# Index keys and key latents turned inside the second index query block, last fill units staged over early scores, low parts of the weights subtracted in quarters

## The chip, the cores and the metric
The kernel runs on one core of a Trainium2 chip. The metric is the device time of one execution in microseconds (us), the median of several runs. TensorE is called PE here, VectorE DVE, ScalarE ACT, GpSimd POOL and the queue of SyncE SP. PSUM (`ps`) is used as 8 banks of 128 x 512 float32.

## The reference
One decoder layer over 1024 tokens of width 1024: an attention branch and a state space branch side by side, merged, then an MLP. What matters here is the attention branch:

```
proj = h @ w_in          # q, kv_lat, q_idx, k_idx, w_idx, z, xbc, dt, g_att, g_ssd
c_kv  = rms_norm(kv_lat); k_idx = rms_norm(k_idx)
# per block of 128 queries:
score[t, s] = sum_h w_idx[t, h] * relu(q_idx[t, h] . k_idx[s])     # 8 heads of 64, causal
keep the 256 keys with the highest score of each query
softmax attention over the kept latents, k = c_kv W_uk, v = c_kv W_uv
```

The first two blocks of 128 queries see at most 256 keys and need no selection.

## The kernel before
Every large product is made of three matmuls in fp32r, hi x hi, hi x lo and lo x hi, where hi is a float32 rounded to fp32r and lo is what is left of it. So each weight block of 1024 x 256 is loaded by SP into `raw[s]` (two buffers, s = n % 2), POOL copies it to `w_hi[s]` (L576) and subtracts to get `w_lo[s]` (L578), and PE waits for both in `w_wait` (L642, semaphore `w_split`). PE gives the buffer back with `w_used`; SP loads the next block into `raw[s]` once `w_split` has counted the block before (L378). There are 90 such splits.

A feature-major block (`fm_block`, L648) runs over k = 0 to 7 with twelve 128x512 matmuls each into four banks. In order of PE's program, from 100 us on:
- the latents and the small columns by token (`kv_token`, `tm_token`), which DVE scales into `ckv_tm` and `kidx_tm`;
- two blocks of index queries, `fm_block(2, 0)` and `fm_block(3, 1)` (L729 to L731). ACT copies each head to `q_idx` (L1244) and DVE subtracts the low part into the other half of the partitions (L1690), in the order heads 0 to 3, keys, heads 4 to 7;
- 8 transposes of `kidx_tm` into banks 0 and 1 (L735), after the second block. ACT makes `k_idx` hi (L1241), DVE lo (L1685);
- four sixteenths of the first q block (`first_q_part`, L738) in banks 0 to 3, then the logits of the index (L756 to L770): ten groups of 8 heads in banks 4 to 7, each followed by another sixteenth. ACT takes the relu (L1252) into four `relu_buf` slots, DVE multiplies by the head's weight and adds up in `score` (L1703, L1705);
- 16 transposes of `ckv_tm` into banks 4 to 7 (L775), after the last relu; ACT makes `ckv_hi` (L1256), DVE `ckv_lo` (L1711) in front of its top-k; PE runs two more sixteenths and waits for them before the next block (L789);
- 15 more blocks for q, k, v, gates, B and C and half of the state space gate. ACT evacuates each two banks as a unit u into `spill[u % 4]` and stores it (`unit`, L1258). The last four, units 40 to 43, go to `last_spill`, which lies over the scores of blocks 4 to 7, so ACT waits with them until top-k has ended (L1297, released at L1802).

Meanwhile DVE runs top-k (L1755 to L1765): three pairs of query blocks, 32 rounds of max and match_replace each. Then attention starts on PE (L873 to L883): scores of head 0 for block t into `ps`, DVE adds the mask (L1781, into `prob`, whose first two buffers lie at 8 and 12 KB of the scores' place), ACT takes the exponential (L1310), PE transposes (L865) into `probT`, and so on. Between the first four positions stand the matmuls of the cumulated decay (L878, L879), whose results DVE takes at L1809, behind a wait for the last units' stores (L1807).

Later, at the end of the state space branch, DVE scales eight sums of squares (L1919), ACT takes the root (L1503), DVE scales `zy` (L1925) and PE turns it (`y_turn`, L889) amid the first output block, for which DVE also makes `a_lo` (L1852).

Of the kernel before, what the change touches and what calls it, by code (L numbers as in the profile page):

```python
# [60 lines left out]
def hybrid_block(nc, x, c, ada_w, ada_b, norm_g, w_in, kv_norm_g, kidx_norm_g, w_uk, w_uv, conv_w, conv_b,  # L61
# [51 lines left out]
    NC = DFF // WC  # L113
    N_ALL = N_MLP + 2 * NC

# [69 lines left out]
    last_spill = [place(f"last_spill{i}", [P, SEQ], F32, R1 + (16 + 4 * i) * K) for i in range(4)]  # L185
# [67 lines left out]
    with ctx:  # L253
# [103 lines left out]
        FREE_BLOCKS = TOPK // P  # L357
# [15 lines left out]
        def _(sp):  # L373
            def load(n, src, dst=None, turn=None, per=0):
                s = n % 2
                if n >= 2 or turn is not None:

                    sp.wait_ge(w_split[s], n // 2 + (0 if turn is None else turn * (per // 2)))  # L378
                dst = raw[s][:, :].rearrange(W3, c=WC) if dst is None else dst
                sp.dma_start(dst, src).then_inc(raw_in[s], 16)  # L380
# [162 lines left out]
        def _(pool):  # L543
# [94 lines left out]
        def _(pe):  # L638
# [3 lines left out]
            def w_wait(n, extra=0):  # L642
                pe.wait_ge(w_split[n % 2], n // 2 + 1 + extra)
# [108 lines left out]
            pe.wait_ge(qi_split, 5)  # L752
            w_wait(4)
            for part in range(4):
                first_q_part(part)
            part = 4  # L756
            pe.wait_ge(qi_split, 9)
            i = 0
            for b in range(FREE_BLOCKS, NT):
                for k0, n in logit_chunks(b):  # L760
                    for h in range(HI):
                        if i >= 4:
                            pe.wait_ge(relu_done, i - 3)
                        o = ps[:, 4 + i % 4, 0:n]
                        q_h = q_idx[:, h, b * P:(b + 1) * P]
                        mm(o, q_h, k_idx[0][:, k0:k0 + n], start=True)
                        mm(o, q_h, k_idx[1][:, k0:k0 + n], stop=True).then_inc(logit_done, 1)
                        i += 1
                    first_q_part(part)
                    part += 1  # L770

            pe.wait_ge(relu_done, LOGITS)
            for r in range(2):
                for t in range(NT):
                    last = nc.tensor.transpose(ps[:, 4 + 2 * r + t // 4, (t % 4) * P:(t % 4 + 1) * P],  # L775
                                               ckv_tm[:, t, r * P:(r + 1) * P], ident[:, :])
            last.then_inc(kv_turned, 1)
# [11 lines left out]
            pe.wait_ge(kv_out_split, 2)  # L789
# [84 lines left out]
            attend(0, range(2), 0)  # L874
# [5 lines left out]
            attend(0, range(2, 4), 0)  # L880
# [292 lines left out]
        def _(act):  # L1173
# [63 lines left out]
            for b in range(2):  # L1237
                act.wait_ge(w_used[b], 2)
                if b:
                    act.wait_ge(kv_turned, 1)  # L1240
                    nc.scalar.copy(k_idx[0][:, :].rearrange("p (a b) -> p a b", a=2), ps[:, 0:2, :]).then_inc(qi_out, 1)  # L1241
                for h in range(4 * b, 4 * b + 4):
                    half, src = q_source(h)
                    nc.scalar.copy(q_idx[half, h, FREE_BLOCKS * P:SEQ], src).then_inc(qi_out, 1)  # L1244
# [9 lines left out]
            act.wait_ge(kv_turned, 2)  # L1254
            for r in range(2):
                nc.scalar.copy(ckv_hi[:, r, :].rearrange("p (a b) -> p a b", a=2), ps[:, 4 + 2 * r:6 + 2 * r, :]).then_inc(kv_out, 1)  # L1256

            def unit(u, func, dst, turn=None, per=0):  # L1258
# [3 lines left out]
                if 4 <= u < 40 or turn is not None:  # L1262

                    act.wait_ge(spilled[b], 16 * (u // 4) + (0 if turn is None else turn * (4 * per)))
# [3 lines left out]
                act.dma_start(dst, stage[:, :]).then_inc(spilled[b] if u < 40 else last_spilled, 16)  # L1268
# [28 lines left out]
            act.wait_ge(topk_step, (NT // 2 - 1) * (2 + 4 * TOPK // 8) + 1)  # L1297
# [322 lines left out]
        def _(dve):  # L1620
# [60 lines left out]

            for n, h in enumerate((0, 1, 2, 3, None, 4, 5, 6, 7)):
# [4 lines left out]
                else:  # L1687
                    half, src = q_source(h)
                    other = slice(DI - half.start, 2 * DI - half.start)
                    ve.tensor_tensor(q_idx[other, h, FREE_BLOCKS * P:SEQ], src,  # L1690
                                     q_idx[half, h, FREE_BLOCKS * P:SEQ].bitcast(F32), ALU.subtract).then_inc(qi_split, 1)
# [17 lines left out]
            for r in range(2):  # L1709
                dve.wait_ge(kv_out, 2)  # L1710
                ve.tensor_tensor(ckv_lo[:, r, :].rearrange("p (a b) -> p a b", a=2), ps[:, 4 + 2 * r:6 + 2 * r, :],  # L1711
                                 ckv_hi[:, r, :].bitcast(F32).rearrange("p (a b) -> p a b", a=2), ALU.subtract).then_inc(kv_out_split, 1)

# [3 lines left out]

            rows8 = [P, NT, NS]

            def every_chunk(row):  # L1720
                return row[:, :].rearrange("p (o h) -> p o h", o=1).broadcast_to(rows8)

            V.link(ve.tensor_tensor(dt[:, :, :], dt[:, :, :], every_chunk(dtb_row), ALU.add))
# [78 lines left out]
            dve.sem_inc(topk_step, 1)  # L1802
# [3 lines left out]
            attend(0, range(2, 4), 0)  # L1806
            dve.wait_ge(last_spilled, 16 * 4)  # L1807
# [271 lines left out]
```

## Time and profile before

| what | value |
|---|---|
| median of 3 runs | 2447.12 us (2447.07 to 2447.74) |
| the profiled execution | 2445.2 us |
| its span, first to last instruction | 2443.5 us |
| PE busy | 2335.8 us (96%) |
| DVE busy | 1383.2 us (57%) |
| ACT busy | 721.9 us (30%) |
| POOL busy | 870.2 us (36%) |
| granted TensorE clock, mean | 0.991 of 2.4 GHz |

Times in rows are us from the span's start. Busy time counts instructions in work; a matmul's end is modelled, so two that follow closely overlap. "Idle before" is how long the engine stood before an instruction, and behind the arrow is what ended it.

### The profile page before, as it was taken

Reading aid. Unit: us, or ns where it says so; the run is one execution under the profiler, and the core shown is the slowest. Engines: PE = TensorE matmul, PEld = TensorE weight load, DVE = VectorE, ACT = ScalarE, POOL = GpSimd, SP = SyncE. Lnnn points to the kernel's source line nnn. Section 1 sums busy time; section 2 is a strip of 40 time slices with the busy share of each in tenths; the row PEclk is TensorE's granted clock in tenths of the full one; section 3 lists DMA queues with packets and bytes.
Section 4 is the critical chain, followed back from the end, with each engine's and each line's share of the span. In section 5 each row is a group of like instructions: output and inputs, shape, how many; then the busy total and the mean of one; then the engine's idle time right before and its main releaser. Section 6 shows DMA issues by size and latency. Waiting matters only on the chain.

```text
span 2443.5 us, 31678 instructions
## 1 busy us (share of the span) xinstructions
PE 2335.8 (96%) x12022; PEld 1927.4 (79%) x12022; DVE 1383.2 (57%) x1956; ACT 721.9 (30%) x1360; POOL 870.2 (36%) x360
## 2 busy tenths in 40 slices
PE   3999999998999999999999999999999999999997
PEld 2977878884557988888877788899888888888886
DVE  4249999995657267685867565544632231322315
ACT  5144121105652234434365111034511211212112
POOL 1221233226671352634445233235323322333232
PEclk9999999999999999999999999999999999999999
DMA  7111452215652113141223443334211111111103
GB/s 270 36 35 39 151 181 90 99 61 177 206 165 72 40 61 125 50 141 40 85 102 125 148 145 133 120 104 138 87 52 52 46 40 51 51 51 34 51 34 78
DMA packets 144729, 230.25 MB, mean 94 GB/s; under 512 B 7956, under 2 KB 111732, under 8 KB 143604
## 3 DMA queue, kind: packets, MB, share of 16 engines
q1 hardware_dynamic: 119936, 166.11, 20.7%
q10 hardware_dynamic: 23684, 59.06, 6.3%
q0 software_dynamic: 1008, 3.67, 0.8%
q8 instruction: 71, 1.16, 0.2%
q14 instruction: 30, 0.25, 0.0%
HBM read 176.39 MB, written 52.43 MB: 94 GB/s over the span
## 4 chain that ended last, share of the span: by engine, by line
PE 71%; issue 12%; DVE 11%; ACT 3%; DVEq 1%; DMA 1%; ACTq 0%
PE ps L646 69%; DVE score L1703 2%; DVE score L1765 1%; DVE top L1761 1%; DVE c_out L1873 1%; DVE probT L1798 1%; DVE mod_sum L1641 1%; DVE x_tm L1980 1%; PE ps L865 1%; DVEq L1755 1%; PE ps L964 0%; PE ps L897 0%; DVE a_lo L1631 0%; ACT decay L1490 0%; DVEq L1763 0%
## 5 line engine op out<-in xcount | busy, mean ns | idle before, releaser
L646 PE MATMUL ps<-a_hi,w_hi 128*128 128x512 f32 x1728 | 679.0, 393 | 6.7 <-DVE k_idx_lo L1685 2.4
L646 PE MATMUL ps<-a_lo,w_hi 128*128 128x512 f32 x1728 | 674.8, 391 | 0.0
L576 POOL CAST w_hi<-raw 128x2048 fp32r<-128x2048 f32 x90 | 176.7, 1964 | 1276.2 <-PE ps L646 1045.0
L646 PE MATMUL ps<-a_hi,w_lo 128*128 128x512 f32 x1728 | 544.6, 391 | 0.0
L578 POOL TENSOR_TENSOR w_lo<-raw,w_hi 128x2048 fp32r<-128x2048 f32 x90 | 431.8, 4798 | 7.2
L2009 DVE TENSOR_TENSOR x_tm<-x_tm,ps 128x1024 f32<-128x1024 f32 x120 | 146.6, 1221 | 453.7 <-PE ps L646 453.1
L646 PEld LDWEIGHTS ps<-a_hi,w_hi 128*128 128x128 f32 x1728 | 325.4, 188 | 76.4 <-issue 3.0
L646 PEld LDWEIGHTS ps<-a_hi,w_lo 128*128 128x128 f32 x1728 | 325.4, 188 | 68.1
L646 PEld LDWEIGHTS ps<-a_lo,w_hi 128*128 128x128 f32 x1728 | 325.6, 188 | 65.8
L646 PE MATMUL ps<-w_hi,a_hi 128*128 128x256 f32 (+1 forms) x896 | 260.8, 291 | 8.5 <-ACTq L1547 4.8
L646 PE MATMUL ps<-w_lo,a_hi 128*128 128x256 f32 (+1 forms) x896 | 255.2, 285 | 0.0
L646 PE MATMUL ps<-w_hi,a_lo 128*128 128x256 f32 (+1 forms) x896 | 255.0, 285 | 0.0
L646 PE MATMUL ps<-w_lo,u_hi 128*128 128x512 f32 x512 | 204.5, 399 | 0.0
L646 PE MATMUL ps<-w_hi,u_hi 128*128 128x512 f32 x512 | 202.0, 394 | 0.0
L646 PE MATMUL ps<-w_hi,u_lo 128*128 128x512 f32 x512 | 200.8, 392 | 0.0
L1596 ACT ACTIVATE u_tmp<-ps 128x512 f32<-128x512 f32 x64 | 37.9, 593 | 522.9 <-PE ps L646 522.9
L646 PEld LDWEIGHTS ps<-w_hi,a_hi 128*128 128x128 f32 x896 | 173.9, 194 | 10.7 <-ACTq L1547 5.0
L646 PEld LDWEIGHTS ps<-w_lo,a_hi 128*128 128x128 f32 x896 | 174.0, 194 | 1.4 <-issue 1.4
L646 PEld LDWEIGHTS ps<-w_hi,a_lo 128*128 128x128 f32 x896 | 174.0, 194 | 0.0
L1765 DVE MATCH_REPLACE8 score<-top,score 128x384 f32<-128x384 f32 (+2 forms) x192 | 166.5, 874 | 0.0
L1761 DVE MAX8 top<-score 128x8 f32<-128x384 f32 (+2 forms) x192 | 160.9, 878 | 0.0
L646 PEld LDWEIGHTS ps<-w_hi,u_hi 128*128 128x128 f32 x512 | 96.2, 188 | 24.9
(255 smaller groups left out, 3094.6 us busy)
## 6 DMA issues: line engine op xcount, KB each, us to landing
raw<-in_w_in_dram SPq DMA_DIRECT2D x35, 1024.0 KB, 5.3
ada_raw<-in_ada_w_dram SPq DMA_DIRECT2D x16, 1024.0 KB, 8.7
raw<-in_w_up_dram SPq DMA_DIRECT2D x16, 1024.0 KB, 5.7
raw<-in_w_down_dram SPq DMA_DIRECT2D x16, 1024.0 KB, 4.8
gates<-gate_d SPq DMA_DIRECT2D x12, 1024.0 KB, 4.9
act_raw<-acts_d ACTq DMA_DIRECT2D x20, 512.0 KB, 5.1
ada<-in_ada_w_dram SPq DMA_DIRECT2D x8, 1024.0 KB, 21.3
acts_d<-decay ACTq DMA_DIRECT2D x16, 512.0 KB, 3.9
```

The source lines that it names most:

```text
L576: nc.gpsimd.tensor_copy(hi, src).then_inc(hi_made, 1)
L578: nc.gpsimd.tensor_tensor(lo, src, hi.bitcast(F32), ALU.subtract).then_inc(w_split[s], 1)
L646: return nc.tensor.matmul(o, a, b, start=start, stop=stop)
L865: ins = nc.tensor.transpose(ps[:, 4 + turns % 2, (k % 4) * P:(k % 4 + 1) * P], prob[(t - 3) % 4][:, k * P:(k + 1) * P], ident[:, :])
L1596: nc.scalar.activation(u_tmp[j][:, :], ps[:, banks[j], :], ACT.Relu).then_inc(up_out, 1)
L1641: V.link(ve.scalar_tensor_tensor(mod_sum[:, :], ada0[:, k, :], c_act[:, k:k + 1], mod_sum[:, :], ALU.mult, ALU.add))
L1703: ins = ve.scalar_tensor_tensor(s, r, w, s, ALU.mult, ALU.add)
L1755: with dve.Fori(0, ROUNDS) as i:
L1761: ve.max(top8[j][:, :], pair[j]).then_inc(topk_step, 1)
L1765: ve.match_replace(pair[j], top8[j][:, :], pair[j], TAKEN).then_inc(topk_step, 1)
L1798: ve.tensor_copy(probT[g % 2][:, k0:k0 + m, q0:q0 + P], ps[:, 4 + turns % 2, 0:m * P].rearrange("p (k q) -> p k q", k=m)).then_inc(pt_out, 1)
L2009: ins = ve.tensor_copy(o, part) if first else ve.tensor_tensor(o, o, part, ALU.add)
```

## The change
Four things are changed.
- PE turns the keys and the first half of the latents at k = 3 of the second index query block, and the second half at k = 5, into banks 0 to 3, which the first block has left. ACT and DVE make their high and low parts before heads 4 to 7. The 16 transposes, copies and subtractions behind the logits are gone. `q_idx` keeps only the queries from 256 on, `ckv_hi` moves and `ckv_lo` lies in the first 8 KB of the scores' place, which the scores of blocks 0 and 1 would take and nobody uses.
- Two sixteenths of the first q block stand ahead of the logits instead of four, and PE waits for the banks of heads 4, 5 and 6, 7 apart.
- Units 40 and 41 are staged over the scores of blocks 2 and 3, units 42 and 43 over `ckv_lo`'s place; ACT waits only until top-k's first pair of blocks is through. DVE waits for the stores of 40 and 41 in front of attention, and for those of 42 and 43 in front of its fourth position; PE runs three positions ahead of the decay matmuls instead of two.
- POOL subtracts `w_lo` in four instructions of a quarter each, and all counts of `w_split` are times four. The sum of dt and its bias moves to a place before the index heads.

```diff
+    LO_PARTS = 4
-    q_idx = place("q_idx", [P, HI, SEQ], F32R, R2)
-    ckv_hi = place("ckv_hi", [P, 2, SEQ], F32R, R2 + 16 * K)
-    ckv_lo = place("ckv_lo", [P, 2, SEQ], F32R, R2 + 24 * K)
+    FREE_BLOCKS = TOPK // P
+    q_idx = place("q_idx", [P, HI, SEQ - TOPK], F32R, R2)
+    ckv_hi = place("ckv_hi", [P, 2, SEQ], F32R, R2 + 24 * K)
+    ckv_lo = place("ckv_lo", [P, 2, SEQ], F32R, R1)
-    last_spill = [place(f"last_spill{i}", [P, SEQ], F32, R1 + (16 + 4 * i) * K) for i in range(4)]
+    last_spill = [place(f"last_spill{i}", [P, SEQ], F32, R1 + (8, 12, 0, 4)[i] * K) for i in range(4)]
...
-                nc.gpsimd.tensor_tensor(lo, src, hi.bitcast(F32), ALU.subtract).then_inc(w_split[s], 1)
+                for j in range(LO_PARTS):
+                    c = slice(j * width // LO_PARTS, (j + 1) * width // LO_PARTS)
+                    nc.gpsimd.tensor_tensor(lo[:, c], src[:, c], hi[:, c].bitcast(F32), ALU.subtract).then_inc(w_split[s], 1)
...
-            for b in range(2):
-                pe.wait_ge(kv_read, b + 1)
-                fm_block(2 + b, b).then_inc(w_used[b], 1)
-            pe.wait_ge(qi_split, 4)
-            for t in range(NT):
-                last = nc.tensor.transpose(ps[:, t // 4, (t % 4) * P:(t % 4 + 1) * P], kidx_tm[:, t, :], ident[:, :])
-            last.then_inc(kv_turned, 1)
+            def kv_turns(k):
+                if k == 3:
+                    pe.wait_ge(qi_split, 4)
+                    for t in range(NT):
+                        nc.tensor.transpose(ps[:, t // 4, (t % 4) * P:(t % 4 + 1) * P], kidx_tm[:, t, :], ident[:, :])
+                if k == 5:
+                    pe.wait_ge(qi_split, 5)
+                if k in (3, 5):
+                    r = (k - 3) // 2
+                    for t in range(NT):
+                        last = nc.tensor.transpose(ps[:, 2 - 2 * r + t // 4, (t % 4) * P:(t % 4 + 1) * P],
+                                                   ckv_tm[:, t, r * P:(r + 1) * P], ident[:, :])
+                    last.then_inc(kv_turned, 1)
+            pe.wait_ge(kv_read, 1)
+            fm_block(2, 0).then_inc(w_used[0], 1)
+            pe.wait_ge(kv_read, 2)
+            fm_block(3, 1, act_ready=kv_turns).then_inc(w_used[1], 1)
...
-            pe.wait_ge(qi_split, 5)
+            pe.wait_ge(kv_out_split, 2)
             w_wait(4)
-            for part in range(4):
+            for part in range(2):
                 first_q_part(part)
-            part = 4
-            pe.wait_ge(qi_split, 9)
+            part = 2
...
+                        elif i % 2 == 0:
+                            pe.wait_ge(qi_split, 7 + i)
...
-            pe.wait_ge(relu_done, LOGITS)
-            for r in range(2):
-                for t in range(NT):
-                    last = nc.tensor.transpose(...)
-            last.then_inc(kv_turned, 1)
...
-            pe.wait_ge(kv_out_split, 2)
+            pe.wait_ge(relu_done, LOGITS)
             fm_block(5, 1).then_inc(w_used[1], 1)
...
-            attend(0, range(2), 0)
+            attend(0, range(3), 0)
...
-            attend(0, range(2, 4), 0)
+            attend(0, range(3, 4), 0)
...
-            act.wait_ge(topk_step, (NT // 2 - 1) * (2 + 4 * TOPK // 8) + 1)
+            act.wait_ge(topk_step, 2 + 4 * TOPK // 8 + 1)
...
-            dve.sem_inc(topk_step, 1)
+            for b in range(2):
+                dve.wait_ge(spilled[b], 16 * 11)
             attend(0, range(2), 0)
             for b in range(2, 4):
                 dve.wait_ge(spilled[b], 16 * 10)
-            attend(0, range(2, 4), 0)
-            dve.wait_ge(last_spilled, 16 * 4)
+            attend(0, range(2, 3), 0)
+            dve.wait_ge(last_spilled, 16 * 2)
+            attend(0, range(3, 4), 0)
```

## Rows read from the trace of the kernel before

**Rows 1.** Busy table by stretch: length, engines' busy us (instructions), PE clock, DMA share, GB/s
```profile
core 0: us, PE busy (x) PEld busy (x) DVE busy (x) ACT busy (x) POOL busy (x), PEclk, DMA share, GB/s
127.00:149.00 22.00, 22.00 (x100) 18.17 (x99) 3.82 (x4) 3.19 (x4) 6.50 (x2) 1.00 0.15 48
...
227.00:549.00 322.00, 321.25 (x1410) 264.21 (x1408) 321.48 (x589) 45.25 (x44) 91.29 (x28) 1.00 0.32 117
549.00:559.00 10.00, 1.70 (x5) 0.93 (x4) 5.49 (x13) 4.09 (x4) 4.45 (x2) 0.76 0.92 322
```
**Rows 2.** Waits of PE: who waited for whom, us in total, times, longest
```profile
PE ps L646 <- ACT last_spill L1265: 8.3, 2, 7.1
```
**Rows 3.** Chain that ended last, around 149 us: start, us, what
```profile
149.01 0.89 PE ps L735 x8
```
**Rows 4.** Timeline of PE: start, us, engine, line, operation, out<-in, idle before
```profile
152.29 0.50 PE L646 MATMUL ps<-a_hi,w_hi 128*128 128x512 f32 x1 [2.42 <-DVE k_idx_lo L1685]
...
157.88 0.34 PE L646 MATMUL ps<-k_idx_hi,q_idx 128*128 128x384 f32 x1
...
213.24 1.97 PE L775 MATMUL ps<-ident,ckv_tm 128*128 128x128 f32 x16 [0.84 <-ACT relu_buf L1252]
...
219.68 0.50 PE L646 MATMUL ps<-a_hi,w_hi 128*128 128x512 f32 x1 [1.71 <-DVE ckv_lo L1711]
...
548.66 0.39 PE L646 MATMUL ps<-a_hi,w_lo 128*128 128x512 f32 x1
...
556.14 0.58 PE L646 MATMUL ps<-hk,hq 128*128 128x128 f32 x1 [7.09 <-ACT last_spill L1265]
...
569.42 0.70 PE L646 MATMUL ps<-hk,hq 128*128 128x512 f32 x1 [2.08 <-DVE att_stat L1784]
```
**Rows 5.** Timeline of ACT (first row) and DVE, 150 to 226 us
```profile
150.88 3.25 ACT L1244 CAST q_idx<-ps 64x768 fp32r<-64x768 f32 x4
...
152.27 3.91 DVE L1690 TENSOR_TENSOR q_idx<-ps,q_idx 64x768 fp32r<-64x768 f32 x4
158.96 0.42 DVE L1705 TENSOR_SCALAR score<-relu_buf,w_idx 128x384 f32<-128x384 f32 x1 [2.77 <-ACT relu_buf L1252]
159.48 4.95 DVE L1703 SCALAR_TENSOR_TENSOR score<-relu_buf,w_idx,score 128x384 f32<-128x384 f32 x7
...
210.03 5.88 DVE L1703 SCALAR_TENSOR_TENSOR score<-relu_buf,w_idx,score 128x512 f32<-128x512 f32 x7
...
220.33 4.72 DVE L1724 SCALAR_TENSOR_TENSOR acum<-dt 128x256 f32<-128x256 f32 x1
...
225.68 0.49 DVE L1753 TENSOR_TENSOR score<-score,future 128x128 f32<-128x128 f32 x2
```
**Rows 6.** Timeline of POOL, then its group of 128x512 additions (xcount, busy us, mean ns)
```profile
151.14 4.60 POOL L578 TENSOR_TENSOR w_lo<-raw,w_hi 128x2048 fp32r<-128x2048 f32 x1
...
220.10 4.68 POOL L578 TENSOR_TENSOR w_lo<-raw,w_hi 128x2048 fp32r<-128x2048 f32 x1
...
L597 POOL TENSOR_TENSOR ada_raw<-ada_raw 128x512 f32<-128x512 f32 x16 | 20.4, 1272 | 1.3
```
**Rows 7.** Timelines of DVE, ACT, DVE from 552 us; landing of last_spill's stores
```profile
552.16 1.36 DVE L1770 TENSOR_SCALAR bias_bf<-score 128x896 bf16<-128x896 f32 x2
...
557.95 1.02 ACT L1265 ACTIVATE last_spill<-ps 128x1024 f32<-128x1024 f32 x1 [0.42 <-ACT last_spill L1265]
...
564.28 0.69 DVE L1781 CUSTOM_DVE_ANT_0 prob<-ps,bias_bf 128x512 f32<-128x512 f32 x1 [0.79 <-PE ps L646]
...
DMA to landing us min/median/max: 3.3/3.6/3.9
```
**Rows 8.** Timelines of DVE, POOL and PE, 1333 to 1350 us
```profile
1337.25 4.57 DVE L1919 TENSOR_SCALAR stat<-stat 128x8 f32<-128x8 f32 x1
1344.37 1.23 DVE L1852 TENSOR_TENSOR a_lo<-act_raw,a_hi 128x1024 fp32r<-128x1024 f32 x1 [2.55 <-ACT a_hi L1383]
...
1336.33 5.47 POOL L578 TENSOR_TENSOR w_lo<-raw,w_hi 128x2048 fp32r<-128x2048 f32 x1
...
1349.11 1.30 PE L897 MATMUL ps<-ident,zy 128*128 128x128 f32 x5 [7.00 <-issue]
```

More of the change, by code:

```diff
@@ L355, in logit_chunks @@
             return [(i * n // parts, n // parts) for i in range(parts)]
-        FREE_BLOCKS = TOPK // P
         LOGITS = HI * sum(len(logit_chunks(b)) for b in range(FREE_BLOCKS, NT))
@@ L376, in load @@
                 if n >= 2 or turn is not None:
-                    sp.wait_ge(w_split[s], n // 2 + (0 if turn is None else turn * (per // 2)))
+                    sp.wait_ge(w_split[s], (n // 2 + (0 if turn is None else turn * (per // 2))) * LO_PARTS)
                 dst = raw[s][:, :].rearrange(W3, c=WC) if dst is None else dst
@@ L642, in w_wait @@
             def w_wait(n, extra=0):
-                pe.wait_ge(w_split[n % 2], n // 2 + 1 + extra)
+                pe.wait_ge(w_split[n % 2], (n // 2 + 1 + extra) * LO_PARTS)
             def mm(o, a, b, start=False, stop=False):
@@ L1238, in _ @@
                 act.wait_ge(w_used[b], 2)
-                if b:
+                for h in range(4 * b, 4 * b + 4):
+                    half, src = q_source(h)
+                    nc.scalar.copy(q_idx[half, h, :], src).then_inc(qi_out, 1)
+                if b == 0:
                     act.wait_ge(kv_turned, 1)
                     nc.scalar.copy(k_idx[0][:, :].rearrange("p (a b) -> p a b", a=2), ps[:, 0:2, :]).then_inc(qi_out, 1)
-                for h in range(4 * b, 4 * b + 4):
-                    half, src = q_source(h)
-                    nc.scalar.copy(q_idx[half, h, FREE_BLOCKS * P:SEQ], src).then_inc(qi_out, 1)
+                    for r in range(2):
+                        act.wait_ge(kv_turned, r + 1)
+                        nc.scalar.copy(ckv_hi[:, r, :].rearrange("p (a b) -> p a b", a=2), ps[:, 2 - 2 * r:4 - 2 * r, :]).then_inc(kv_out, 1)
             i = 0
@@ L1253, in _ @@
                         i += 1
-            act.wait_ge(kv_turned, 2)
-            for r in range(2):
-                nc.scalar.copy(ckv_hi[:, r, :].rearrange("p (a b) -> p a b", a=2), ps[:, 4 + 2 * r:6 + 2 * r, :]).then_inc(kv_out, 1)
             def unit(u, func, dst, turn=None, per=0):
@@ L1261, in unit @@
                 stage = spill[b] if u < 40 else last_spill[b]
-                if 4 <= u < 40 or turn is not None:
+                if 4 <= u < 42 or turn is not None:
                     act.wait_ge(spilled[b], 16 * (u // 4) + (0 if turn is None else turn * (4 * per)))
@@ L1267, in unit @@
                 act.wait_ge(unit_out, u + 1 + (0 if turn is None else turn * per))
-                act.dma_start(dst, stage[:, :]).then_inc(spilled[b] if u < 40 else last_spilled, 16)
+                act.dma_start(dst, stage[:, :]).then_inc(spilled[b] if u < 42 else last_spilled, 16)
             def fm_units(n, u, func, dst, turns):
@@ L1680, in _, with every_chunk @@
             ins.then_inc(kv_read, 1)
+            rows8 = [P, NT, NS]
+            def every_chunk(row):
+                return row[:, :].rearrange("p (o h) -> p o h", o=1).broadcast_to(rows8)
+            dve.wait_ge(kv_read, 2)
+            V.link(ve.tensor_tensor(dt[:, :, :], dt[:, :, :], every_chunk(dtb_row), ALU.add))
             for n, h in enumerate((0, 1, 2, 3, None, 4, 5, 6, 7)):
@@ L1689, in _ @@
                     other = slice(DI - half.start, 2 * DI - half.start)
-                    ve.tensor_tensor(q_idx[other, h, FREE_BLOCKS * P:SEQ], src,
-                                     q_idx[half, h, FREE_BLOCKS * P:SEQ].bitcast(F32), ALU.subtract).then_inc(qi_split, 1)
+                    ve.tensor_tensor(q_idx[other, h, :], src, q_idx[half, h, :].bitcast(F32), ALU.subtract).then_inc(qi_split, 1)
+                if h is None:
+                    for r in range(2):
+                        dve.wait_ge(kv_out, r + 1)
+                        ve.tensor_tensor(ckv_lo[:, r, :].rearrange("p (a b) -> p a b", a=2), ps[:, 2 - 2 * r:4 - 2 * r, :],
+                                         ckv_hi[:, r, :].bitcast(F32).rearrange("p (a b) -> p a b", a=2), ALU.subtract).then_inc(kv_out_split, 1)
             i = 0
@@ L1708, in _ @@
             dve.wait_ge(relu_used, LOGITS)
[L1709 to L1712, printed above, removed]
             ROUNDS = TOPK // 8
[L1718 to L1723, printed above, removed]
             ve.scalar_tensor_tensor(acum[:, :, :], dt[:, :, :], -1.0, dt[:, :, :], ALU.mult, ALU.max).then_inc(dt_abs, 1)
```

4 lines of the change are left out of this document (1 added, 3 removed).

## The prediction
> **What bounds the kernel now.** I read the table of busy time by stretch first, then the waits of TensorE (PE), then the chain and the engines' rows around each wait. PE works 321.25 of the 322 us from 227 to 549, so a change pays only where it stands still, and it stands for most of 549 to 559 [rows 1]. The waits name the causes [rows 2, 4]: 8.3 us for the last staged fill units, 2.4 for the low part of the index keys, 1.7 for that of the key latents. The longest single one comes at the end of the block: PE runs its last matmul until 549.05 and starts attention at 556.14, 7.09 us later [rows 4]. The cause is two steps back. DVE's top-k ends at 552.16 + 1.36 = 553.52; ScalarE (ACT) may copy the last four units only then, since they are staged where the scores lie, and takes them at 1.45 us each until 558.97; attention's fourth score block is masked at 564.28 and PE has a steady feed from 569.42 [rows 4, 7]. Two chains end here close together: DVE's (logits, top-k) at 553.5 and PE's (projections) at 549.05. The change shortens both, and the later one decides.
>
> **Index block.** The 8 key transposes (0.89 us) and 16 latent transposes (1.97) [rows 3, 4] move into the block that runs from 127.3 to 149.0. They stay PE work, so the block ends at 149.01 + 0.89 + 1.97 = 151.87. ACT's and DVE's copies of what they turn fall into this block, of whose 22 us they work 3.2 and 3.8 [rows 1]. The wait at k = 3 (about 135.4) needs q heads 0 to 3, whose low parts are done 4.8 us into the block, by 132.1. That at k = 5 (about 142.7) needs the keys' low part, which comes the 2.4 us of today's wait behind the turns, by 140. Both cost nothing; without that cover k = 5 would cost up to those 2.4 us. Nothing else is queued behind them on PE but the block itself. The waits of 2.42, 0.84 and 1.71 on PE disappear.
> After 151.87 ACT copies heads 4 to 7 (0.81 each) and DVE subtracts (0.98 each) [rows 5], one copy behind: heads 4, 5 are ready at 154.7, all at 156.65. PE meanwhile does two q parts; four of them ran from 152.29 until the first logit at 157.88, so 1.40 each [rows 4]. So it starts logits 0 and 1 at 154.7 and waits some 1.3 us for the rest. DVE could then start its scores at 156.7 instead of 158.96, 2.26 us sooner.
>
> It will hardly do so. GpSimd (POOL) splits the next weights as soon as this block ends; its low part ran from 151.14 for 4.60 us, 2.1 us behind the block's end [rows 6], and moves to 154.0. Such an instruction holds off DVE: the 128x256 scalar_tensor_tensor that began at 220.33, inside POOL's 220.10 + 4.68, took 4.72 us, and 8 elements at 1337.25 took 4.57, until POOL was done [rows 5, 6, 8]. In quarters of 1.27 [rows 6] (about 1.2 from start to start) the third runs until 157.65, so the first score is done at 158.0; the fourth then goes first, until 159.2; the second score ends at 159.85, against 160.1 before. Gain of DVE's stream: 0.25 us, between 0 (all four quarters ahead) and 2.26 (no collision); I take 0.25, since the rows show the collision. The Trainium skill, SBUF — State Buffer, section "Who interferes with whom", says that a VectorE instruction with two SBUF inputs, or in a 2-port mode, and a GpSimd one lock each other out for the whole instruction, whichever came first. By that rule, which the 4.72 us bears out, the start at 156.7 is lost; without it the whole forecast would be 1.8 us lower.
>
> From here DVE sets the pace (scores back to back until 210.03 + 5.88 = 215.91 [rows 5]), so the whole phase moves by 0.25. Then PE's path: its last logit ended at 213.24 - 0.84 - 1.40 = 211.0, now 210.75. Five q parts are left instead of three (two first instead of four), 7.0 us, so the next block starts at 217.8 against 219.68 [rows 4]: 1.9 gained. The work up to 549.05 has no slack [rows 1], so PE's projections end at **547.15**.
> DVE's path: from the last score at 215.91 to the first top-k row at 225.68 it spends 9.77 us [rows 5], of which the latents, the dt sum (now earlier, in an idle stretch) and the 4.72 go. Left are acum, by estimate 0.45 (384 elements take 0.62 of such an instruction, the first seven scores 4.95 between them), since POOL's split starts only with the next block, and the bias writes with 225.68 - 225.05 = 0.63: 1.1. So 8.65 + 0.25 sooner, and top-k ends at **544.6**. PE's chain is the later by 2.5 us.
>
> **Last units.** Units 40 and 41 are now staged over scores that the first top-k pair has finished, 42 and 43 over the dead latents; ACT no longer waits for top-k's end. 40 and 41 go out during the last block; their added wait is for stores of a block before. 42 and 43 follow at 547.2 and 548.65, the store of 43 is issued at 549.7 and lands 3.3 to 3.9 us later [rows 7], at 553.35. New behind that: DVE waits for units 42 and 43 ahead of the fourth mask, with ACT's fourth exponential, the decay sums and the masks 5 and on queued behind it. PE can compute its scores from 547.2; the fourth, after the two sums, is there by 552 at the full clock, so the landing is last. Mask 4 starts at 553.35 against 564.28 [rows 7]: **10.9 us gained**. From there to the steady feed it is the same 5.14 us (569.42 - 564.28), ACT, DVE and PE in turn. Bounds: 9.3 if ACT's shift alone carried through (unit 43 from 557.95 to 548.65), 12.8 if the score stream got its 2.26. SP's ada loads start with the block's end, 1.9 us sooner, and attention 10.9 sooner, so POOL's ada sums lose 9 us of their lead; no wait for them stands in today's list on PE, and I take the lead to be long enough.
>
> **Quarters.** Per split, 4 x 1.27 - 4.6 = about 0.4 us more on POOL, some 90 times, beside PE blocks of 149.0 - 127.3 = 21.7 us (half, 11 us, in the output projection, whose blocks have half the columns) of which cast and low part take 2.1 + 4.6 [rows 6]: hidden; it would cost PE only past some 4 us a split. Where DVE has four or more blocked instructions in a row (conv, x1), POOL takes every other turn and the stall is the same in sum: 0. One border gains. At 1337.25 DVE stands 4.57 us behind the low part that really began at 1337.2 (the 5.47 from 1336.33 include the wait for DVE) [rows 8]; with quarters it stands 1.3, 3.3 less. The next subtraction, which ran from 1344.37 to 1345.6, would come at 1341.1 [rows 8], meets the last quarter there, waits until 1342.2 and ends at 1343.5. So PE's wait, 7.00 us until 1349.11, ends 2.1 sooner; bounds 0 (alternation eats it) and 3.3. I take **2.1**.
>
> **Sum.** 10.9 + 2.1 = 13.0. The profiled execution took 2445.2 us (span 2443.5), 1.9 under the median of 2447.1; against it the changed one would be 2432.2, and the median **2434.1**.
>
> **Rivals.**
> - **A slow clock at the new seam.** The granted clock averages 0.76 in 549 to 559 after PE's idle 7 us [rows 1], so part of it is at 1.2 instead of 2.4 GHz. Now PE has small pieces and waits of 1 to 2 us from 547 to 558.5; if the clock falls late in this stretch, the dense work behind it runs at half speed. For: in the rows PE starts dense work only at 569.42 - 10.9. Against: its idle is in pieces. Price 2 to 5 us: 2437.5. 18%. The Trainium skill, TensorE: Matmul & The Clock Gate, part 1, calls the lower clock the default, released by activity; that makes this rival possible, no more.
> - **The border's gain is eaten** by alternating quarters: 10.9 alone, 2436.2. 12%.
> - **No collision at the first scores:** 12.8 + 2.1, 2432.2. 8%.
> - **Nothing comes through.** The fourth mask waits for a store stuck behind 2 MB of ada loads that now start 2.5 us before it, by 11 us, or top-k stays last at 553: only the border's 2.1 is left, 2445. For: the DMA engines are 92% busy there [rows 1]. Against: under this same load stores landed within 3.9 us. 7%.
> - **Slower: a quarter costs POOL nearly what the whole did.** Then a split takes 2.1 + 4 x 4.6 = 20.5 us: just under the 21.7 of a large block, but 9.5 over the 11 of the eight output blocks, 76 us, and the time is 2447 - 13 + 76 = 2510. It costs from a quarter of about 2.2 us (2.1 + 8.8 = 10.9) and ends slower than before from 2.9. Against: 128x512 takes 1.27 on POOL [rows 6]. With milder forms, such as DVE's instructions stretching each quarter, 5%.
>
> **How the numbers follow.** Forecast 50% (own range 2431.5 to 2437), rivals as given. 0.2% is 4.9 us, about what a measurement can tell from no change: faster 88%, same 7%, slower 5%. The range takes in the first three rivals and the bounds of both terms: 2430.5 to 2439.5.
>
> **What the changed profile should show.** No PE wait for k_idx_lo or ckv_lo; first score near 158, stalled; acum under 0.6 us; top-k's last row near 544.6, PE's last projection near 547.2; wait for last_spill under 3 us; fourth mask near 553.4, waiting for a DMA; the eight-element scaling near 1337 - 11 in about 1.3 us. It is wrong if top-k ends after the projections, if the fourth mask comes past 556, or if PE is seen waiting for w_lo.

## The result, and the profile after

The changed kernel takes **2426.1 us** (four executions: 2422.4 to 2432.3), against 2447.4 (2447.1 to 2448.0) on the same chip: ratio 0.9915, 95% interval 0.9894 to 0.9936, a gain of 21.4 us where 13.0 was forecast. The time lies below the range. Two things ask for an explanation: the size, and the spread of 10 us. The kernel before spreads by 1 us in these four executions and by 2.9 to 4.5 us in the ten or eleven that were timed with each group of experiments below. The profiled execution is the slowest of the four: 2432.3 us, span 2430.5, hardly off the forecast for it (2432.2). That agreement is an accident, as the rows show.

PE does the same work in the same order outside the index phase, so the same instruction can be looked up in both timelines. The difference of its two starts is the lead, the time won so far. The starts of PE in the kernel before, where [rows 4] and [rows 8] don't have them:
```profile
51.12 5.41 PE L694 MATMUL ps<-ident,x_tm 128*128 128x128 f32 x24 [4.61 <-ACT h_tmp L1187]
331.16 0.49 PE L646 MATMUL ps<-a_hi,w_hi 128*128 128x512 f32 x1 [0.49 <-issue]
1328.46 1.52 PE L646 MATMUL ps<-state,c_fm 128*128 128x512 f32 x2 [2.64 <-DVE zy L1915]
1366.48 0.47 PE L646 MATMUL ps<-a_hi,w_hi 128*128 128x512 f32 x1 [0.89 <-issue]
1681.57 0.58 PE L646 MATMUL ps<-w_hi,a_hi 128*128 128x256 f32 x1 [4.78 <-ACTq L1547]
1741.98 0.63 PE L694 MATMUL ps<-ident,x_tm 128*128 128x128 f32 x4 [1.19 <-ACT h_tmp L1187]
```
and the same in the changed kernel (start, us, what, idle before; the third row is the start of the block that [rows 4] has at 219.68):
```profile
49.86 7.32 PE L697 MATMUL ps<-ident,x_tm 128*128 128x128 f32 x32 [3.02 <-ACT h_tmp L1196]
155.25 0.45 PE L649 MATMUL ps<-k_idx_hi,q_idx 128*128 128x384 f32 x1 [1.01 <-DVE q_idx L1705]
215.65 0.39 PE L649 MATMUL ps<-a_hi,w_hi 128*128 128x512 f32 x1
326.53 0.49 PE L649 MATMUL ps<-a_hi,w_hi 128*128 128x512 f32 x1 [0.46 <-issue]
544.26 0.82 PE L649 MATMUL ps<-hk,hq 128*128 128x128 f32 x4
547.00 1.60 PE L649 MATMUL ps<-hk,hq 128*128 128x384 f32 x2 [1.92 <-DVE att_stat L1791]
557.10 2.76 PE L649 MATMUL ps<-hk,hq 128*128 128x512 f32 x4 [4.37 <-DVE att_stat L1791]
561.21 1.13 PE L649 MATMUL ps<-hk,hq 128*128 128x512 f32 x2 [0.71 <-DVE att_stat L1791]
1318.70 2.04 PE L649 MATMUL ps<-state,c_fm 128*128 128x512 f32 x2 [2.64 <-DVE zy L1924]
1337.10 1.30 PE L906 MATMUL ps<-ident,zy 128*128 128x128 f32 x5 [4.83 <-issue]
1355.18 0.47 PE L649 MATMUL ps<-a_hi,w_hi 128*128 128x512 f32 x1 [0.89 <-issue]
1670.46 0.58 PE L649 MATMUL ps<-w_hi,a_hi 128*128 128x256 f32 x1 [4.98 <-ACTq L1555]
1728.15 0.63 PE L697 MATMUL ps<-ident,x_tm 128*128 128x128 f32 x4 [1.19 <-ACT h_tmp L1196]
```
The lead: 1.3 us at the first block, 4.0 at 219.68, 4.6 at 331, **8.2** at the steady feed of attention (569.42, now 561.21), 9.8 at 1328, 12.0 at 1349.11, 11.3 at 1366, 11.1 at 1681, 13.8 at 1742 (of which 0.8 is lost after PE's last matmul). Index phase and seam (the border between projections and attention, near 550 us) give 6.9 of it instead of 10.9, the border near 1340 gives 1.3, and 4.7 comes from places for which the forecast had zero: 1.3 at the first block, 1.6 in the state space groups between 569 and 1328, 1.2 right behind the wait at 1681, 1.5 at the second border near 1730, less the 0.8 at the end. The 1.2 is no shorter wait: PE found a granted clock of 0.67 in the 9 us from 1681.5 before and 0.83 from 1670.4 now. So the profiled sum is right by errors that cancel, and the other three executions are 6 to 10 us faster still.

**The seam.** DVE's rows there and ahead of it:
```profile
396.03 2.67 DVE L1777 TENSOR_SCALAR bias_bf<-score 128x640 bf16<-128x640 f32 x2
398.74 1.40 DVE L1748 TENSOR_TENSOR dec<-dec,dta 128x256 f32<-128x256 f32 x1
544.87 1.36 DVE L1777 TENSOR_SCALAR bias_bf<-score 128x896 bf16<-128x896 f32 x2
556.16 0.69 DVE L1788 CUSTOM_DVE_ANT_0 prob<-ps,bias_bf 128x512 f32<-128x512 f32 x1 [5.85 <-DMA gate_d<-last_spill]
```
and the issues of DMA between 540 and 560 us (count, KB each, median us to landing; `ada_raw` are weights of 1 MB that SP loads from the end of the projections on, two of them ahead of the stores):
```profile
ada_raw<-in_ada_w_dram SPq DMA_DIRECT2D x3, 1024.0 KB, 6.3
gate_d<-last_spill ACTq DMA_DIRECT2D x2, 512.0 KB, 8.8
```
The fourth mask waited for the store, as forecast, but until 556.16: the two stores, issued at 545.52 and 546.96, land 8.5 and 9.0 us later, where those of before took 3.3 to 3.9 [rows 7]. From the mask to the steady feed it is 5.05 us (forecast: 5.14).

**The merge at 1660 us** (where the two branches join and the rows called x1 are stored), which the forecast didn't mention. SP:
```profile
1659.08 0.37 SPq L381 DMA_DIRECT2D raw<-in_w_out_dram  x1
1659.49 2.25 SPq L502 DMA_DIRECT2D x_in<-in_x_dram  x4
```
ACT:
```profile
1660.30 0.34 ACTq L1579 DMA_DIRECT2D out_dram<-x_tm  x1
1668.59 1.15 ACT L1587 ACTIVATE x_tm<-x_tm,stat 128x1024 f32<-128x1024 f32 x1 [4.29 <-DMA out_dram<-x_tm]
```
and the landing of the four x1 stores:
```profile
DMA to landing us min/median/max: 2.6/3.1/8.2
```
The fourth x1 store is issued 1.2 us behind 1 MB of weights, and 0.8 and 0.2 us behind the first two of four residual rows of 512 KB; the other two follow it. It lands after 8.2 us. ACT waits for it, ACT's evacuation of the next merge bank is queued behind, and PE waits 4.98 us for that evacuation (row 1670.46).

### The profile page after: what moved, and what is told of

It is laid out like the page before. It is cut to its first block, busy times and chain, and to the rows that moved or that the text cites. A ratio compares the mean times of both kernels' runs of the same rounds, so it can differ in the third digit from the quotient of the medians.

```text
span 2430.5 us, 31946 instructions
## 1 busy us (share of the span) xinstructions
PE 2335.0 (96%) x12022; PEld 1924.2 (79%) x12022; DVE 1328.7 (55%) x1956; ACT 723.3 (30%) x1360; POOL 950.8 (39%) x630
## 4 chain that ended last, share of the span: by engine, by line
PE 89%; DVE 6%; issue 2%; ACT 2%; DMA 1%; ACTq 0%; DVEq 0%
PE ps L649 86%; DVE score L1722 2%; DVE probT L1805 1%; DVE mod_sum L1649 1%; PE ps L906 1%; PE ps L874 1%; PE ps L973 1%; DMA gate_d<-last_spill 0%; ACT decay L1498 0%; PE ps L697 0%; DVE a_lo L1861 0%; DMA out_dram<-x_tm 0%; DVE x_tm L1989 0%; DVE x_tm L1991 0%; DMA rows_b<-in_ssm_norm_g_dram 0%
## 5 line engine op out<-in xcount | busy, mean ns | idle before, releaser
L581 POOL TENSOR_TENSOR w_lo<-raw,w_hi 128x512 fp32r<-128x512 f32 (+1 forms) x360 | 520.2, 1477 | 7.2
L649 PEld LDWEIGHTS ps<-w_hi,a_hi 128*128 128x128 f32 x896 | 173.1, 193 | 10.9 <-ACTq L1555 5.2
```

Source lines behind the costliest of these rows:

```text
L581: nc.gpsimd.tensor_tensor(lo[:, c], src[:, c], hi[:, c].bitcast(F32), ALU.subtract).then_inc(w_split[s], 1)
L649: return nc.tensor.matmul(o, a, b, start=start, stop=stop)
```

## The experiments

All kernels were timed beside the kernel before (medians 2447.2 to 2448.0, so a difference between runs of different groups carries up to 0.8 us from that alone). "Profiled" is the execution that left the trace. The questions: why does the time vary, and what is each part worth?

**1. The changed kernel again**, unaltered.

> The changed kernel unaltered, to see how its time varies from execution to execution (2422.4 to 2432.3 us, against 2447.1 to 2448.0 for the kernel before). Theory S (store): the store of unit 43 competes with ada loads issued 2.5 us ahead of it, and its landing varies; it set DVE's fourth mask at 556.16 in the profiled execution, 9.2 us after its issue at 546.96. If it lands after 4 us in another execution, the mask starts near 551 and the span is 5 us shorter. So profiled landing time and span go together: a span near 2424 should show the fourth mask near 551, one near 2430 near 556. Rival C (clock): the granted clock of 0.989 or 0.995 goes with the span (2430.5, 2424.7 and 2423.8 at 0.989; 2420.6 at 0.995), with stretches at 1.2 GHz of different length and place; then the mask's time and the span don't go together. Rival B (beginning): the starts differ by the weights' first loads; then all rows are shifted alike from 130 us on.

2426.8 us, ratio 0.9919 [0.9906, 0.9933]. The executions: 2424.7, 2426.4, 2426.8, then 2433.0 and the profiled 2435.1: two groups, at least 6 us apart. In the profiled one the fourth mask again waited for the store (PE's longest wait for att_stat is 4.9) and PE again waited at the merge, 5.4 us. The mean granted clock was 0.991 in it and 0.989, 0.994, 0.995 in the three shorter ones, so clock and time don't go together (against rival C).

**2. Ada loads behind the last fill stores.**
```
             sp.wait_ge(w_used[1], N_SSM // 2)
+            sp.wait_ge(last_spilled, 16 * 2)
             load_ada(0)
```


> The changed kernel with SyncE waiting for both last stores before its first ada load. Theory S: unit 43's store lands 3.3 to 3.9 us after its issue, the fourth mask starts near 551 in every execution, the spread of times falls to about 1 us, and the time is 2422 or a little less. Rivals C and B: landing as short, but the spread of 10 us and the median of 2426 stay. If the ada sums on GpSimd then come late, a wait for them appears on PE and the time is above 2426.

2424.1 us, ratio 0.9898 [0.9883, 0.9913]. The fourth mask:
```profile
551.13 0.69 DVE L1789 CUSTOM_DVE_ANT_0 prob<-ps,bias_bf 128x512 f32<-128x512 f32 x1 [0.81 <-issue]
```
and the stores' group in the table of DMA:
```profile
gate_d<-last_spill ACTq DMA_DIRECT2D x2, 512.0 KB, 2.7
```
The landing falls from 8.8 to 2.7 us and the mask comes 5.03 sooner: the first half of theory S is shown. The second half falls: executions of 2419.1, 2421.2, 2427.1 and 2428.1 spread as widely as before. So the fill store isn't what makes the executions differ; what it costs is measured in run 10. The ada sums bore the delay: PE's waits for ada_sum are 0.3 us.

**3. Low part in one instruction** (LO_PARTS = 1).

> The changed kernel with the low part in one instruction again. By the prediction quarters are worth 2.1 us (2.1 at the border at 1337, 0.25 at the first scores): 2426 becomes 2428.5. Rival Q (quarters worth more, at many places): the differences seen between 985 and 1366 us (gain grows from 8.1 to 11.3) and in 1681 to 1752 (11.1 to 13.8) are theirs, 5.5 us: 2431 to 2432.

2439.2 us, ratio 0.9966 [0.9954, 0.9978], all six executions within 1.6 us. Quarters are worth 12.4 us beside the unaltered kernel of run 1, six times the forecast of 2.1, and without them the spread is gone. Waits of PE (total, times, longest), low part whole:
```profile
PE ps L906 <- issue: 8.3, 1, 8.3
PE ps L697 <- ACT h_tmp L1196: 6.2, 4, 4.1
PE ps L649 <- ACTq L1555: 4.5, 1, 4.5
PE ps L649 <- DVE zy L1924: 4.5, 3, 2.6
PE ps L649 <- DVE a_lo L1639: 1.7, 2, 1.1
```
and in quarters (the changed kernel):
```profile
PE ps L649 <- ACTq L1555: 5.0, 1, 5.0
PE ps L906 <- issue: 4.8, 1, 4.8
PE ps L697 <- ACT h_tmp L1196: 4.2, 2, 3.0
PE ps L649 <- DVE zy L1924: 2.6, 1, 2.6
PE ps L649 <- DVE a_lo L1639: 0.6, 1, 0.6
```
Four waits are shorter with quarters: at the border near 1337 by 3.5, at the first block by 2.0, for the groups' zy by 1.9, for a_lo by 1.1. A shorter wait is not yet time won. By the starts of PE the quarters give 1.1 us at the first block, 1.6 for zy, 2.2 at the border and 1.4 for a_lo. At the border PE without quarters had the full clock in the 11 us ahead (1.00 granted, instead of 0.84) and reached its wait sooner, so that the wait was longer by more than the quarters win. With 1.1 us across the seam, where the kernel without quarters had the slower clock (0.64 from 551.5 to 564, the other 0.86), less 0.3 at the merge and 0.7 behind the last matmul, it is 6.4 us of span (2436.9 against 2430.5). The other 6 are in none of the profiled executions.

**4. Quarters alone**, in the kernel before.

> The kernel before with the quarters alone. Prediction: the border at 1337 gains 2.1 us and the score phase 0 to 2: 2445 (2443 to 2447). Rival Q: 5 us or more, 2442 or less. DVE's first scores should show the stall in pieces of 1.3 us instead of one of 4.7.

2438.6 us, ratio 0.9953 [0.994, 0.9967], 9 us below the kernel before: rival Q holds. Two levels again, 2433.1 and 2433.3 against 2438.6, 2438.8 (profiled) and 2439.2. So the levels come with quarters whatever the seam is.

**5 to 7. Quarters in one stretch only**, all other low parts whole.
```
-                for j in range(LO_PARTS):
+                for j in range(parts):   # shortened: 4 where weight n is in the stretch, else 1
...
```


> Quarters only in the splits ahead of attention (weights 0 to 20), all later low parts in one instruction; beside the kernel with no quarters (2439.2 us, all executions within 1.6) and with all (2426.4, executions between 2422.4 and 2435.1). Theory P (the profile shows all of it): what quarters give stands in the profiles, 1.1 to 1.4 us here at the first block: 2438, one level, within 1.6 us. Rival H (a step hidden from the profiled executions): executions fall into two levels some 5.5 us apart, as 2433.2 and 2438.8 in the kernel before with quarters; if its cause is in this stretch, this kernel shows both levels, or the lower alone: 2432.5.

Weights 0 to 20: 2439.0 us, ratio 0.9965 [0.9952, 0.9978]; executions 2436.2 to 2440.0. In its profile the first block is 1.4 us ahead of the kernel without quarters, but the time is not: what is won there is within the spread.

> Quarters only in the splits from attention's end to the last SSM group (weights 21 to 38). Theory P: 1.6 us, the two waits for zy of 0.9 and 0.7 that go from TensorE's list: 2437.6, one level. Rival H, if the cause is here: a second level 5.5 us lower, near 2432.

Weights 21 to 38: 2436.3 us, ratio 0.9957 [0.9944, 0.9969]; 2435.1 to 2437.8, one level, 2.9 below the kernel without quarters. The two intervals overlap; in the profiles the waits for zy give 1.6 us of PE's lead.

> Quarters only in the splits of the output projections and the MLP (from weight 39 on). Theory P: the border at 1330 to 1355 gives 2.1 us and the second border near 1700 gives 1.1 to 1.5: 2435.5 to 2436, one level. Rival H, if the cause is here: two levels, the lower near 2430.

Weights from 39 on: 2430.0 us, ratio 0.993 [0.9918, 0.9942]: 2426.7, 2427.0, 2427.1, 2432.9, 2436.3 and the profiled 2439.9. Only this kernel of the three spreads (13 us), and its shortest executions are 12 us below the kernel without quarters. The hidden step is behind weight 38: output projection, merge or MLP. The only long wait of PE there that depends on a landing is the one at 1670. That gave theory D, that two transfers race at the merge.

**8. Merge weights and residual rows behind the fourth x1 store.**
```
             for j in range(8):
+                if j == 7:
+                    sp.wait_ge(x_landed[3], 32)
                 load(N_OUT + j, cols(w_out[0], j % 4 * WC))
```


> The changed kernel with SyncE holding its last merge weights and the four residual rows queued behind them until the fourth x1 store has landed. Theory D (a race of transfers at 1660): in the profiles of the kernels with quarters that store is issued about 1 us behind 1 MB of weights and 1 to 2 MB of rows, lands 8.2 to 8.7 us later instead of 2.6, and TensorE stands 5.0 to 5.4 us for it (L1555); the fast executions are those in which the store goes first. Then the hold makes every execution fast: store landed after 2.6 us, the PE wait at most 1 us, no second level, 2422 to 2424, spread below 3 us but for the store of unit 43. Rival C (clock or something else in the tail): landing short, but two levels and a median of 2426 stay.

2425.7 us, ratio 0.9912 [0.9897, 0.9926]; the four executions, the profiled one among them, lie within **1.0 us** (2425.2 to 2426.2). The landing of the x1 stores:
```profile
DMA to landing us min/median/max: 2.6/2.7/3.4
```
and PE's wait for the merge (total, times, longest):
```profile
PE ps L651 <- ACTq L1557: 0.6, 1, 0.6
```
The upper group is gone and the time is that of the lower group, of which single executions went down to 2422.4. The profile gains what the unprofiled executions had: its PE runs 6.6 us ahead of the changed kernel's profile from 1690 us on, 5.7 of them won at the merge. Of the 5.7, 4.4 is the shorter wait, and 1.3 comes right behind it, where PE found the full clock in the 9 us from its start instead of 0.83.

**9. The same hold, low part whole.**

> The same hold, with the low parts in one instruction (that kernel without the hold: 2439.2 in all executions, TensorE waits 4.5 us at the same place). Theory D: the hold takes most of the 4.5 us here too, 2435 to 2436. If the time stays near 2439, the wait there has the stalled x1 rows of VectorE (5.75 us behind one low part) as its own cause, and only quarters free both.

2432.7 us (2432.4 to 2435.0), ratio 0.9942 [0.9929, 0.9954], PE's wait at the merge 1.2 us. So late stores cost 6.5 us in the kernel without quarters too, and in every execution, since the ranges don't touch (without the hold 2438.6 to 2440.2). In the two profiles 4.8 of it is won at the merge; the rest stands at no place in them. Theory D had expected 3 to 4 us. Quarters beside the hold: 2432.7 - 2425.7 = **7.0 us**. PE's starts in the two profiles with the hold show the same places as run 3: 1.2 at the first block, 1.6 for zy, 2.1 at the border, 1.4 for a_lo.

**10. Both holds.**

> Both holds: ada loads behind the last fill stores, merge weights behind the x1 stores, with quarters. Theories S and D together: 4 to 5 us below 2424.1 in the executions that were slow there, none in the fast ones: 2419 to 2420 in every execution, spread about 2 us; the profiled span near 2421. If only one of the two races matters: 2424.

**2421.4 us**, ratio 0.9895 [0.988, 0.9909], executions 2420.7 to 2422.2. It beats both kernels: 26.6 us below the one before and 4.7 below the changed one. Against the hold of run 8 alone it is 4.4 (spans of the profiles: 2418.9 and 2423.3), and that is what the fill store had cost. The hold at the merge by itself takes little off the median (2426.1 to 2425.7), for most executions had won that race; what it takes away is the upper group.

**11. The last units wait for top-k's end again.**
```
-            act.wait_ge(topk_step, 2 + 4 * TOPK // 8 + 1)
+            act.wait_ge(topk_step, (NT // 2 - 1) * (2 + 4 * TOPK // 8) + 1)
...
+            dve.sem_inc(topk_step, 1)
```


> The changed kernel, but ScalarE again waits for top-k's end before the last four units; all else stays. In the kernel before, unit 43's copy ended 5.4 us and the fourth mask started 10.8 us behind top-k's end (553.5, 559.0, 564.3). With top-k's end at 546.2 the mask would come at 557.0: 0.8 us behind the 556.16 of the changed kernel, since its four stores go out after the ada loads have passed. So if theory S holds, the early staging brings only 0.8 us as long as its stores collide: 2427. Rival (the staging carries the gain, as predicted): 5 to 9 us more, 2431 to 2435.

2431.8 us (2429.3 to 2438.6), ratio 0.9938 [0.9926, 0.995]: 5.0 slower than the changed kernel in run 1, so my 0.8 was wrong and the staging does carry gain. Where:
```profile
548.95 1.65 PE L649 MATMUL ps<-hk,hq 128*128 128x128 f32 x4 [4.42 <-ACT last_spill L1273]
556.62 1.65 PE L649 MATMUL ps<-hk,hq 128*128 128x384 f32 x2 [6.03 <-DVE att_stat L1791]
```
Even the first mask waits now, for the stores of units 40 and 41 (they lie where the probabilities go), until 556.1; the fourth comes at 561.67. I had counted from the last copy and left this wait out. The four stores, issued 2.9 to 7.3 us behind the first of the two ada loads, landed after 7.2, 7.0, 6.8 and 6.6 us. It isn't a clean undoing of the step, for in the kernel before those areas were free.

**12. Eight parts**, ada loads held.

> Eight parts instead of four, with the ada loads behind the last stores (that kernel with four: 2424.1, executions 2419.1 to 2428.1). If what counts is how long one GpSimd instruction holds VectorE off at the borders, a piece of 256 elements stands 0.7 us instead of 1.3, and the borders give 0.5 to 1.5 us more: 2423. If GpSimd's own time becomes the bound (8 instructions take over 5.6 us, some 1 us more for each split beside 21.7 us blocks), nothing is lost beside large blocks: 2424; slower only if the pieces of 256 cost over 1 us each.

2425.6 us, ratio 0.9912 [0.9899, 0.9925], executions 2424.6 to 2427.1. All x1 stores land within 3.5 us, without a hold at the merge (the fourth is now issued 2.5 us ahead of the weights), but no gain against four parts is left: 2424.1 with the same hold, and 2421.4 with both, which is the fair comparison, since there too no store is late. Why, in POOL's row:
```profile
1695.72 12.02 POOL L582 TENSOR_TENSOR w_lo<-raw,w_hi 128x256 fp32r<-128x256 f32 x8
```
and PE's:
```profile
1655.76 0.38 PE L650 MATMUL ps<-w_hi,a_hi 128*128 128x256 f32 x1 [1.08 <-POOL w_lo L582]
1707.89 0.77 PE L650 MATMUL ps<-a_hi,w_hi 128*128 128x512 f32 x1 [2.95 <-POOL w_lo L582]
```
Eight alternations with DVE stretch a low part to 12 us, and PE waits for it: the slower rival of the prediction, in small.

## Why the prediction was off, point by point

**Right.** The waits for k_idx_lo and ckv_lo are gone. The first logits wait 1.01 us for the other heads (forecast 1.3). The first score is held until a quarter of POOL's ends, acum takes 0.43 (forecast 0.45), in DVE's rows:
```profile
155.22 1.28 DVE L1724 TENSOR_SCALAR score<-relu_buf,w_idx 128x384 f32<-128x384 f32 x1
156.61 5.79 DVE L1722 SCALAR_TENSOR_TENSOR score<-relu_buf,w_idx,score 128x384 f32<-128x384 f32 x7
213.94 0.43 DVE L1731 SCALAR_TENSOR_TENSOR acum<-dt 128x256 f32<-128x256 f32 x1
```
It was done at 156.50, forecast 158.0 less the 1.3 us of lead at the start. The exclusive lock that the Trainium skill describes (SBUF — State Buffer, "Who interferes with whom") held again: the first score took 1.28 us beside POOL's quarters where it had taken 0.42 alone [rows 5], and DVE's and POOL's instructions took turns. The next block started at 215.65, a lead of 4.0, of which 1.3 from the start: 2.75 where 1.9 was forecast (score stream 0.7 instead of 0.25, five q parts 6.8 us instead of 7.0).

The border, DVE's scaling of eight elements and a_lo:
```profile
1327.54 1.25 DVE L1928 TENSOR_SCALAR stat<-stat 128x8 f32<-128x8 f32 x1
1331.34 2.25 DVE L1861 TENSOR_TENSOR a_lo<-act_raw,a_hi 128x1024 fp32r<-128x1024 f32 x1 [2.55 <-ACT a_hi L1391]
```
What PE found in the 10 us behind its wait, in the kernel before (columns as in [rows 1]):
```profile
1349.00:1359.00 10.00, 9.89 (x48) 8.56 (x49) 6.88 (x5) 2.23 (x2) 0.00 (x0) 0.81 0.26 104
```
and in the changed kernel:
```profile
1337.00:1347.00 10.00, 9.90 (x42) 8.39 (x43) 6.87 (x4) 2.23 (x2) 0.00 (x0) 0.73 0.21 84
```
The scaling took 1.25 us instead of 4.57, a_lo met the last quarter (2.25 instead of 1.23) and the wait ended 12.0 - 9.8 = 2.2 sooner; forecast 2.1. Of it 0.7 was given back: PE found 0.73 of the full clock instead of 0.81, more of the stretch at 1.2 instead of 2.4 GHz.

The rival of a slow clock at the new seam did not come true: the granted clock was 0.59 from 557.0 to 561.2, most of it at 1.2 GHz, but 1.00 in the 10 us of dense work behind 561.2, and mask to feed took no longer than before. No wait for an ada sum appeared on PE.

**Wrong, step 1: the landing of the last fill store** ("lands 3.3 to 3.9 us later"). The mechanism was right (the landing ends the wait), the term was too small: it was 9.2 us (issue 546.96, mask 556.16), 5.5 more than the 3.65 taken. Since the issue itself came 2.7 sooner than forecast (549.7), the mask was late by 2.8. The argument "under this same load stores landed within 3.9 us" compared unlike things: before, SP issued its two ada loads at 549.1 and 549.5, which landed 5.3 and 7.8 us later, and the four stores came 5.6 to 9.9 us behind the first, when the 2 MB were nearly through; now they come 1.1 and 2.5 us behind. What went with a late landing was how much of the loads was still under way at the issue, not the share of busy DMA engines: run 11 lies between (6.6 to 7.2 us), run 2 has no competitor (2.7 us). The rival "stuck behind 2 MB" had the mechanism, and priced it at 11 us with a chance of 7%; it was 5.5. The Trainium skill (DMA: Bandwidth & Descriptors, "Issuing engines are not separate DMA queues") says that transfers issued by different engines run on the same 16 DMA engines and interleave; the 2.7 against 8.8 us agree with it.

**Wrong, step 2: the end of top-k** ("544.6", 2.5 ahead of the projections). It came at 546.23, 1.8 behind them (PE was done at 544.4). DVE had moved by 9.85 us there (405.88 to 396.03) and POOL, bound to PE's blocks, by 4.6; so the bias writes between two top-k pairs fell into a low part: 2.67 us for two instructions that took 1.09 before, 1.40 for an addition of 0.43, and 0.85 more for the same pair at 287 us; 3.4 lost in all. I had taken the stretch up to 549 as rigid on DVE, though its instructions beside POOL's were exactly of the kind that the prediction treated at two other places. PE's 1.92 us at 547.00 are a wait for the first mask, which starts 0.2 us behind top-k's end. At the fourth mask it cost nothing here, since that waited for the store.

**Wrong, step 3: quarters "One border gains", elsewhere 0.** This is the largest, and by itself it puts the time below the range: 12.4 us instead of 2.1 (run 3). It failed in two ways.
First, single DVE instructions on the critical chain stand behind a low part at more places than the one that I priced: the gain factors of the first block (8 elements: 1.78 us before, 0.47 now), y_t and zy in two groups, a_lo at the second border. By PE's starts these give 1.3 + 1.6 + 1.5 us against the kernel before. I looked for them only where PE's wait was long.
Second, in the chain of x1 rows "POOL takes every other turn and the stall is the same in sum" was beside the point. DVE's row behind the low part took 5.75 us with the low part whole (run 3's kernel):
```profile
1656.99 5.75 DVE L1989 SCALAR_TENSOR_TENSOR x_tm<-x_tm,stat,row 128x1024 f32<-128x1024 f32 x1
```
while POOL did
```profile
1657.04 4.62 POOL L581 TENSOR_TENSOR w_lo<-raw,w_hi 128x2048 fp32r<-128x2048 f32 x1
```
In quarters POOL's four pieces took 8.01 us (from 1651.04), DVE's row 2.43. So the rows' results leave earlier and the low part ends later, and each releases a transfer: DVE's rows the x1 stores, POOL's last piece the next weights with the residual rows behind them. Whole, the loads were issued 5.2 us ahead of the fourth store (1661.69, 1666.94) and 2.5 ahead of the third, and both stores landed late, after 7.1 and 7.3 us; in quarters the loads come 1.2 us ahead of the fourth (1659.08, 1660.30) and behind the third, which lands in 2.6. The reading that fits the times is that at 1.2 us the fourth may also come through first and land in 2.6 us instead of 8.2. That is the spread, and the 6 us that the profiled execution did not win. The chain of waits of the kernel before named the store, as the piece "1672.24 7.38 DMA out_dram<-x_tm", and PE's list had 4.8 us behind it; I took both as given and not as something the change could move.

**What is shown and what isn't.** Shown: with the loads held there is no upper group and the time is that of the lower one (runs 8 and 10, four executions each, within 1.0 and 1.6 us); the race lies behind weight 38 (runs 5 to 7), and its late stores cost 6.5 us in the kernel without quarters (run 9); the fill store costs 4.4 (run 10 against 8). Not shown: the order of store and loads in a short execution. In all six kernels with four parts behind weight 38 and no hold at the merge the profiled execution had the late store, each time issued 1.21 to 1.23 us behind the weights. So the trace has not caught the issues changing places, and that the order stays while the transfers are served otherwise is as possible. Open as well: what tips it, 1.7 of the 6.5 us of run 9, and 0.6 us that PE gains between 219 and 331 us, which the kernel without quarters gains too.

**The sum as it should have been**, by the runs: last fills and turns with both low parts whole 8.6 (run 3: 2447.8 - 2439.2), quarters without the race 7.0 (run 9 against 8), the merge race 6.5 where it is won. These make 22.1, against 21.4 measured for the mixture of executions. They are differences of measured times, so this is where the gain lies and not a second forecast that came true.

## What to carry to other kernels

When a change shifts when an engine ends, list every DMA whose issue hangs on it, and compare its issue time with those of the transfers that somebody waits for: a store that followed a bulk load by 1 to 3 us landed 5 to 6 us later here than one ahead of it. Hold the bulk load, which has slack, behind the small store, which has none. Two such waits, of one and two lines, took the time from 2426.1 to 2421.4 us and the spread from 10 us to 1.6; in the kernel without quarters the second alone was worth 6.5 us. And cutting a long instruction that locks out another engine pays by the latency of the single short instructions behind it (8 elements fell from 4.57 to 1.25 us), so count them on the whole critical chain, not at the longest wait, and count starts, not waits. Cut no finer than the engine's own slack allows: eight parts were 4.2 us slower than four where no store was late.

## What the runs showed of the hardware

A 512 KB store took 2.6 to 2.7 us from issue to landing with no load issued in the 10 us before it, and 7.5 to 9.0 at the seam with 2 MB of loads issued on another queue up to 2.5 us before. In between lie the four stores of run 11, issued 2.9 to 7.3 us behind such loads, with 6.6 to 7.2 us (the second load itself took 10.0 us there, 7.8 in the kernel before); and those of the kernel before and of run 4, 5.2 to 9.9 us behind them, with 3.3 to 4.3. I had not expected the profiled execution to be a poor witness: all six traces showed the late store, while by their times some 17 of the 24 other executions of those kernels were in the lower group. With the loads held (runs 8 and 10) the profiled execution was the shortest of its kernel, so profiling alone does not make an execution slow. Where the times of one kernel spread and its trace doesn't explain it, look for two transfers that are issued close together by different engines, as here.
